# Head decays from running sums in a two-layer trunk kernel: what is computed where, and in which order

## The chip, the cores and the metric

The kernel runs on one core of one Trainium2 chip. The metric is device time in microseconds (us) of one execution, as the median of several runs. The core has five engines that run side by side and meet only at semaphores: TensorE (PE, matmuls; its weight load is shown apart as PEld), VectorE (DVE), ScalarE (ACT), GpSimd (POOL) and SyncE (SP, which here only issues DMAs). TensorE writes its products to PSUM, eight banks of 128 partitions x 512 float32.

## The reference, cut to what matters

Input x is 256 tokens x 2048 channels, and there are two layers (DEPTH = 2). Each layer is

```
h = rmsnorm(x, norm_w)
proj = h @ w_in                      # u, s5_gate, z, xbc, dt, q, k, v, att_gate, merge logits
y_s5  = s5_mixer(u, ...) * silu(s5_gate)
y_ssd = ssd_mixer(z, xbc, dt, ...)
y_att = window_attention(q, k, v, att_gate, ...)
x = x + (sum_b sigmoid(g_b) * (y_b @ w_branch_b)) @ w_out
```

and the part that the change touches most is the decay between two tokens of one head in the ssd mixer (16 heads):

```
dt = softplus(dt_raw + dt_bias)
a = dt * -exp(a_log)                             # [head, token], negative
segsum(a)[l, s] = cumsum(a)[l] - cumsum(a)[s]    # for l >= s, else -inf
scores = (C_l . B_s) * exp(segsum(a))
y = scores @ (x * dt) + ... + x * d_skip
```

The S5 mixer is a diagonal complex recurrence. Its eight tiles of 128 channels need a table of sines and cosines each.

## The kernel before, in words

**Weights as a stream.** All large weights come as 148 slabs per layer (128 x 2048 float32, 1 MB) through four buffers `raw`. SyncE loads slab j+4 once TensorE has done slice j (`load`, L374). ScalarE rounds a slab to `w_hi` (`hi`, L685), VectorE forms the rest `w_lo = raw - w_hi` in the memory of `raw` (`lo`, L1002), and TensorE multiplies three times: high x low, low x high, high x high (`prod3`, L1628). ScalarE and VectorE work three slabs ahead (LEAD = 3). A slice of TensorE is one slab: 48 matmuls of 256 columns (`pair`, L1634) or 24 of 512 columns (`block`, L1661).

**Order by hand.** Every engine's program is written out by slices. What is not the stream (called side work below) is put between the slices of each engine by `if n == ...`, and the engines meet at named marks: `W.wait(LV, "in2")` waits for VectorE's mark `in2` of this layer, `W.wait(MP, "ys1", 1)` for TensorE's mark `ys1` of the tile before. Each engine takes its instructions strictly in its own order, so whatever stands behind a waiting instruction waits too.

**First slices (n = 0 to 15 of a layer).** Slices 0 to 3 give B and C, 4 and 5 k, 6 and 7 v (written to the banks `by` and `bs`), 8 to 15 u. The norm of x is not applied to x: it scales the results. So TensorE starts on unscaled x, sums the squares by a matmul with ones after slice 0 (mark `ss`, L1711; GpSimd adds up the squares in `ssum` before, L498), VectorE and ScalarE make 1/sqrt of it (`rstd`, L1060, L699), and VectorE multiplies each slice's bank with it (mark `in<n>`, L1213). The two banks `mm` take turns, so slice n needs `in<n-2>`. VectorE's side work here: `s5_angles` behind slice 0, `rtok` (token norms turned to columns), `s5_gamma` and `s5_powers` behind slice 2, `c_gamma` behind 3 and 4, `conv` behind 4 to 7, `dt_softplus` (L1163) behind 6. TensorE's `lam_T` (behind slice 5) needs `powers` and `rtok`. GpSimd begins the first S5 tile when `c_gamma` is done (`gamma_end`). SyncE issues, behind the load of j = 13, the store of the first half of u, waits for it to land, and then 17 loads for the first S5 tile: one for `bd`, eight `lam`, eight `ut` (`s5_in`, L380). `kv` (L1756), the first S5 product on TensorE, needs them two slices after slice 15.

**Middle slices (16 to 47)** hold z, xs, q and the attention gate, and four S5 tiles.

**Gate slices (48 to 95).** A loop of four rounds, I = 0 to 3, of 12 slices each. A round holds one S5 tile and two mix tiles c = 0 and 1 (six slices each, t = 0 to 5); a mix tile is two ssd heads and two attention heads. The steps of a mix tile that matter here, before the change:
- VectorE: `conv` of xs and its SiLU `xc` (t = 0); `q_v` and `xdt` (t = 1); a `newton` step on the q norm and `qn` (end of t = 1); then `lo`, `q_c` and `st_make(0)` (t = 2), which multiplies decays `ex` with `gm`; `sc`, maxima and `st_make(1)` (t = 3).
- ScalarE: `sum_decays` (L819) writes three 128 x 128 matrices `m1`, masks scaled with a token's decay, for head 0 at t = 0 and for head 1 at t = 2; `head_exp` (L827) takes exp of what TensorE makes of them; `sines` (L767) of the round's S5 tile at s = 0; `inv_sqrt` at t = 1.
- TensorE: `diff(0)` (L1822) behind t = 2 and `diff(1)` behind t = 3: three float32 products of `m1` with a triangle of ones, which sum the decays between tokens; `ssd_y(0)` and the attention scores `a1(0)` behind t = 3; `a2`, `a3` later.
- GpSimd: `parameters(0)`, the S5 tile of the next round (`s5_tile`, with `values(0)` inside), `parameters(1)`, `values(1)` (L614 to L656). They copy the tile's few numbers into `cur`.
- SyncE: in rounds 0 to 2, behind the load of s = 5, the 17 loads of `s5_in` for the next round.

**Last slices (96 to 147)**: S5 gate, GLU, branch projections, output projection. The change leaves them alone.

## Time and profile before

| | us |
|---|---|
| median of 3 runs | 1973.13 |
| range of the runs | 1972.01 to 6226.87 |
| the profiled execution, its own time | 1972.46 |
| its span, first to last instruction | 1970.7 |
| TensorE matmul busy in it | 1914.7 (97%) |
| VectorE busy | 1335.0 (68%) |
| ScalarE busy | 953.2 (48%) |
| GpSimd busy | 519.0 (26%) |
| mean granted TensorE clock | 0.993 of full speed |

The span is the profiled execution; about 1.8 us lie around it. "Busy" of TensorE counts overlapping matmuls, whose durations are longer than the distance from one start to the next, so cost per matmul is read from start times. The largest of the 6226.87 us is one of the three runs, the other two are within 1.2 us of each other.

### The profile page before, as it was taken

What the parts mean: (1) busy time and instruction counts of PE and PEld (TensorE: products, weight loads), DVE (VectorE), ACT (ScalarE), POOL (GpSimd) and SP (SyncE); (2) the same over time, 40 slices, a digit from 0 to 9 for tenths busy, and PEclk for the clock granted to TensorE, in tenths of its full rate; (3) what the DMA queues carried; (4) which work ended last, traced back from release to release, by engine and by line L of the source; (5) the groups of instructions that cost most, each with busy time, mean ns of one, the idle gap of its engine ahead of it and who ended that gap; (6) DMA issues with size and microseconds to landing.
All of it is one profiled execution on the core that took longest, in us unless ns stands there. A gap on an engine that the chain in (4) does not pass through costs nothing.

```text
span 1970.7 us, 38606 instructions
## 1 busy us (share of the span) xinstructions
PE 1914.7 (97%) x13680; PEld 1706.1 (87%) x13680; DVE 1335.0 (68%) x1733; ACT 953.2 (48%) x1164; POOL 519.0 (26%) x578
## 2 busy tenths in 40 slices
PE   5999999999999999999999999999999999999998
PEld 5999999777777799889999999997777778988898
DVE  6957656777776658666578566667776866676656
ACT  5334333666656554333444344455656565543334
POOL 4215444152342000002312353424241410000033
PEclk9999999999999999999999999999999999999999
DMA  6445555545454447666554555555545454566656
GB/s 259 166 161 206 181 184 189 174 161 190 153 172 166 152 168 256 229 233 211 198 176 168 196 184 178 180 198 174 169 159 173 154 173 171 182 260 234 229 192 207
DMA packets 79444, 372.82 MB, mean 189 GB/s; under 512 B 20560, under 2 KB 27216, under 8 KB 40528
## 3 DMA queue, kind: packets, MB, share of 16 engines
q1 hardware_dynamic: 76560, 359.99, 52.5%
q0 software_dynamic: 1088, 6.80, 0.9%
q10 hardware_dynamic: 1696, 4.72, 0.6%
q8 instruction: 60, 0.98, 0.2%
q14 instruction: 40, 0.33, 0.0%
HBM read 351.80 MB, written 21.76 MB: 190 GB/s over the span
## 4 chain that ended last, share of the span: by engine, by line
PE 83%; DVE 7%; issue 4%; DMA 3%; POOL 1%; ACT 1%; SPq 1%; DVEq 0%; POOLq 0%; ACTq 0%
PE mm L1673 13%; PE mm L1675 13%; PE mm L1674 13%; PE mm L1630 12%; PE mm L1632 12%; PE mm L1631 12%; DMA raw<-in_stream 2%; DVE w_lo L1005 2%; PE by L1836 1%; PE b L1827 1%; PE b L1772 1%; PE b L1848 1%; PE b L1847 1%; POOL ssum L498 1%; DVE qh L1009 1%
## 5 line engine op out<-in xcount | busy, mean ns | idle before, releaser
L691 ACT ACTIVATE w_hi<-raw 128x2048 fp32r<-128x2048 f32 x299 | 571.7, 1913 | 695.8 <-DMA raw<-in_stream 686.3
L1005 DVE TENSOR_TENSOR w_lo<-raw,w_hi 128x2048 fp32r<-128x2048 f32 x299 | 695.9, 2328 | 231.2 <-ACT w_hi L691 222.2
L1630 PE MATMUL mm<-h_lo,w_hi 128*128 128x256 f32 x2240 | 645.6, 288 | 29.6 <-DVE w_lo L1005 15.0
L1632 PE MATMUL mm<-h_hi,w_hi 128*128 128x256 f32 x2240 | 638.6, 285 | 0.0
L1631 PE MATMUL mm<-h_hi,w_lo 128*128 128x256 f32 x2240 | 638.6, 285 | 0.0
L1630 PEld LDWEIGHTS mm<-h_lo,w_hi 128*128 128x128 f32 x2240 | 434.7, 194 | 34.6 <-issue 25.3
L1631 PEld LDWEIGHTS mm<-h_hi,w_lo 128*128 128x128 f32 x2240 | 434.8, 194 | 1.4 <-issue 1.0
L1632 PEld LDWEIGHTS mm<-h_hi,w_hi 128*128 128x128 f32 x2240 | 434.5, 194 | 0.0
L1673 PE MATMUL mm<-w_lo,h_hi 128*128 128x512 f32 x768 | 317.8, 414 | 0.0
L1675 PE MATMUL mm<-w_hi,h_lo 128*128 128x512 f32 x768 | 301.3, 392 | 0.0
L1674 PE MATMUL mm<-w_hi,h_hi 128*128 128x512 f32 x768 | 300.0, 391 | 0.0
L1673 PEld LDWEIGHTS mm<-w_lo,h_hi 128*128 128x128 f32 x768 | 144.5, 188 | 38.1 <-issue 9.4
L672 POOL TENSOR_TENSOR ssum<-ssum,proj 128x256 f32<-128x256 f32 x32 | 73.2, 2289 | 384.7 <-ACT proj L974 357.2
L1675 PEld LDWEIGHTS mm<-w_hi,h_lo 128*128 128x128 f32 x768 | 144.3, 188 | 32.2
L1674 PEld LDWEIGHTS mm<-w_hi,h_hi 128*128 128x128 f32 x768 | 144.8, 189 | 27.2
L1673 PE MATMUL mm<-w_lo,ys 128*128 128x512 f32 x384 | 150.3, 391 | 0.5 <-DVE tmp L1560 0.5
L1675 PE MATMUL mm<-w_hi,ys 128*128 128x512 f32 x384 | 149.5, 389 | 0.0
L1674 PE MATMUL mm<-w_hi,ys 128*128 128x512 f32 x384 | 149.5, 389 | 0.0
L1009 DVE TENSOR_TENSOR proj<-mm,rstd 128x256 f32 (+1 forms) x104 | 47.0, 452 | 134.6 <-PE mm L1632 134.0
L1673 PEld LDWEIGHTS mm<-w_lo,ys 128*128 128x128 f32 x384 | 72.1, 188 | 16.3 <-DVE tmp L1560 0.9
L1675 PEld LDWEIGHTS mm<-w_hi,ys 128*128 128x128 f32 x384 | 72.1, 188 | 15.0
L1674 PEld LDWEIGHTS mm<-w_hi,ys 128*128 128x128 f32 x384 | 72.1, 188 | 14.7
(313 smaller groups left out, 2280.1 us busy)
## 6 DMA issues: line engine op xcount, KB each, us to landing
raw<-in_stream SPq DMA_DIRECT2D x300, 1024.0 KB, 4.8
gscr<-gt SPq DMA_DIRECT2D x48, 256.0 KB, 6.0
gin<-gscr SPq DMA_DIRECT2D x24, 512.0 KB, 5.7
bd<-in_bdense SPq DMA_DIRECT2D x16, 384.0 KB, 5.3
lam<-lscr SPq DMA_DIRECT2D x128, 32.0 KB, 2.7
x_old<-out POOLq DMA_DIRECT2D x2, 2048.0 KB, 9.3
out<-proj ACTq DMA_DIRECT2D x8, 512.0 KB, 6.4
proj<-in_x SPq DMA_DIRECT2D x4, 512.0 KB, 8.5
```

The source lines that it names most:

```text
L498: e.tensor_tensor(ssum[:], ssum[:], proj[:, 16 + m, :], ALU.add).then_inc(x_sum, 1)
L672: e.tensor_tensor(ssum[:], ssum[:], proj[:, bass.ds(I * 4 + (16 + j), 1), :].rearrange("p a b -> p (a b)"), ALU.add).then_inc(x_sum, 1)
L691: e.activation(w_hi[:, j % RAW, :], raw[:, j % RAW, :], ACT.Copy).then_inc(hi_done, 1)
L1005: e.tensor_tensor(w_lo[:, j % RAW, :], raw[:, j % RAW, :], w_hi[:, j % RAW, :].bitcast(F32), ALU.subtract).then_inc(lo_done, 1)
L1009: return e.tensor_tensor(out, a, b, op)
L1630: e.matmul(out, whi, xlo, start=start, stop=False)
L1631: e.matmul(out, wlo, xhi, start=False, stop=False)
L1632: return e.matmul(out, whi, xhi, start=False, stop=stop)
L1673: e.matmul(mm[:, tok, :], xhi[:, rows], w_lo[:, j % RAW, w], start=first and k == 0, stop=False)
L1674: e.matmul(mm[:, tok, :], xhi[:, rows], w_hi[:, j % RAW, w], start=False, stop=False)
L1675: ins = e.matmul(mm[:, tok, :], xlo[:, rows], w_hi[:, j % RAW, w], start=False, stop=last and k == QUAD - 1)
L1772: ins = e.matmul(b4[rows, r * 256 + j * CH:r * 256 + j * CH + CH], bw[rows, r, j * 64:j * 64 + 64], ut[rows, j, :], start=True, stop=True)
```

## The change

1. Behind slice 13 TensorE makes running sums of the decays of all 16 heads at once (four small float32 products into bank `b7`, mark `cs`); ScalarE copies them out, once as rows per head (`csr`, stored to DRAM as `cscr`) and once negated as columns per token (`csb`). In the gate slices GpSimd loads a tile's two rows, spread over all 128 partitions (`crow`, 256 KB per tile, after a wait for VectorE's `dd1` of the tile before), and copies its columns into `cur`. VectorE forms the differences at t = 0 with six instructions (`decays`), ScalarE takes one exp over both heads at t = 1. `sum_decays`, `head_exp` and `diff` go, and `m1` with them; `ex` holds both heads.
2. `sines` in the gate slices moves from s = 0 to s = 2.
3. The product `ss` moves behind slice 1, `rtok` behind slice 3 (on VectorE to n = 4), the rstd work to n = 0 behind `lo`/`hi` of that slice. Slices 2 and 3 write to the banks `by` and `bs`; slices 4 and 5 wait for `in0`, `in1`, slice 6 for `in2` and `in3`.
4. VectorE: `c_gamma` moves from n = 3, 4 to n = 8, 9, `dt_softplus` from n = 6 to n = 11.
5. SyncE: the first S5 tile's `bd` and `lam` loads go behind the load of j = 11, its `ut` loads behind that of j = 15.

The diff, cut to its core:

```diff
@@ SyncE
-                    e.dma_start(bd[:], ob).then_inc(s5_w, 16)
+                    if weights:
+                        e.dma_start(bd[:], ob).then_inc(s5_w, 16)
...
                         e.dma_start(uscr[0:4].rearrange("i p t -> p i t"), proj[:, U:U + 4, :]).then_inc(u_out[0], 16)
+                    if j == 11:
                         e.wait_ge(lam_out, n_lam)
-                        W.settle()
+                        s5_in(0, 0, values=False)
+                    if j == 15:
                         e.wait_ge(u_out[0], n_u)
-                        s5_in(0, 0)
+                        s5_in(0, 0, weights=False)
@@ GpSimd, parameters(c)
+                        MG.mark(e.tensor_copy(cc[:, 5:11].rearrange("p (b d) -> p b d", b=3), csb[:, :, bass.ds(i * 2, 2)]), "cur3")
...
                         MG.mark(e.tensor_scalar(cc[:, 27:28], cc[:, 27:28], 0.5, 0.0, ALU.mult, ALU.add), "cur4")
+                        e.wait_ge(cs_out, e.snap((L + 1) * 16))
+                        W.wait(MV, "dd1", 1)
+                        W.settle()
+                        e.dma_start(crow[:], cscr[bass.ds(i * 2, 2), :].unsqueeze(0).broadcast_to([P, 2, TOK])).then_inc(cs_in, 16)
@@ ScalarE
-                inv_sqrt(LA, "rs", rstd[:], sv[:, 1, :], sv[:, 0, :], lambda: W.wait(LV, "rs_v"))
-
                 nb = start(L, 0)
                 for n in range(16):
                     hi(nb, n + LEAD)
                     if n == 0:
+                        inv_sqrt(LA, "rs", rstd[:], sv[:, 1, :], sv[:, 0, :], lambda: W.wait(LV, "rs_v"))
...
+                    if n == 15:
+                        W.wait(LP, "cs")
+                        LA.mark(e.activation(csr[0:16, :], b7[0:16, 0:TOK], ACT.Copy), "cs_row")
+                        LA.mark(e.activation(csb[:, 0:2, :], b7[:, TOK:TOK + 32].rearrange("p (a b) -> p a b", a=2), ACT.Copy, scale=-1.0), "cs_own")
+                        LA.mark(e.activation(csb[:, 2, :], b7[:, TOK + 32:TOK + 48], ACT.Copy), "cs_rest")
+                        W.wait(LA, "cs_row")
+                        e.dma_start(cscr[:], csr[0:16, :]).then_inc(cs_out, 16)
...
+                        def decay_exp():
+                            W.wait(MV, "dd1")
+                            MA.mark(e.activation(ex[:], ex[:], ACT.Exp), "ex")
...
                             if t == 1:
                                 inv_sqrt(MA, "q", qh[:], rq[:], rv[:], lambda: W.wait(MV, "q_v"))
+                                decay_exp()
...
-                                sum_decays(0)
-                            if s == 0:
+                            if s == 2:
                                 sines()
-                            if t == 2:
-                                head_exp(0)
-                                sum_decays(1)
                             if t == 3:
                                 att_exp(0)
-                                head_exp(1)
@@ VectorE
+                    if n == 0:
+                        lo(nb, LEAD)
+                        W.wait(LP, "ss")
+                        LV.mark(e.tensor_scalar(sv[:, 0, :], b4[:, 0:TOK], 1.0 / D_MODEL, EPS, ALU.mult, ALU.add), "rs_v")
+                        newton(LV, "rs", rstd[:], sv[:, 1, :], sv[:, 0, :])
+                    bank = (by, bs)[n - 2][:, 0:TOK] if n in (2, 3) else mm[:, n % 2, 0:256]
...
-                    if n in (3, 4):
-                        c_gamma(n - 3)
+                    if n in (8, 9):
+                        c_gamma(n - 8)
...
-                    if n == 6:
+                    if n == 11:
                         dt_softplus()
...
+                        def decays():
+                            e.wait_ge(cs_in, turn_in + 16 * c)
+                            W.wait(MG, "cur3")
+                            W.wait(MV, "ST1", 1)
+                            for h in range(2):
+                                for q, (at_r, b) in enumerate(((0, 0), (P, 2), (P, 1))):
+                                    ins = e.tensor_scalar(ex[:, h, q * P:q * P + P], crow[:, h, at_r:at_r + P], cc[:, 5 + 2 * b + h:6 + 2 * b + h],
+                                                          0.0, ALU.add, ALU.min)
+                                MV.mark(ins, f"dd{h}")
...
                                 MV.mark(e.scalar_tensor_tensor(xc[:], tt[:], 1.0, xc[:], ALU.add, ALU.mult), "xc")
+                                decays()
@@ TensorE
+                    if n == 13:
+                        W.wait(LV, "dta")
+                        W.wait(LV, "k_v")
+                        for b in range(2):
+                            e.matmul(b7[0:16, b * P:b * P + P], dta[:, 0, b, :], C("tri", P), start=True, stop=True)
+                        e.matmul(b7[:, TOK:TOK + 32], C("tri", P), dta[:, 0].rearrange("p a b -> p (a b)"), start=True, stop=True)
+                        LP.mark(e.matmul(b7[:, TOK + 32:TOK + 48], C("strict"), dta[:, 0, 0, :], start=True, stop=True), "cs")
...
-                        def diff(h):
-                            W.wait(MA, f"m1_{h}2")
-                            W.wait(MA, f"ex{h ^ 1}", 0 if h else 1)
-                            if not h:
-                                W.wait(MV, "xdt")
-                            e.matmul(b6[:, 0:256], m1[:, 0, :], C("tri"), start=True, stop=False)
-                            e.matmul(b6[:, 128:256], m1[:, 1, :], C("tri", P), start=False, stop=True)
-                            MP.mark(e.matmul(b6[:, 256:384], m1[:, 2, :], C("tri", P), start=True, stop=True), f"diff{h}")
```

The scratch `tq` now shares memory with `rq`, and `xdt` with `tt`, with the waits for it.

## Rows read from the trace of the kernel before

**Rows 1.** The page, part 1: busy time, share of the span, instructions.
```profile
PE 1914.7 (97%) x13680; PEld 1706.1 (87%) x13680; DVE 1335.0 (68%) x1733; ACT 953.2 (48%) x1164; POOL 519.0 (26%) x578
```

**Rows 2.** Waits of TensorE: waiter, releaser, us in total, times, longest.
```profile
PE mm L1630 <- DVE proj L1009: 11.0, 4, 3.7
PE by L1836 <- DVE stt L1009: 10.6, 6, 1.8
PE b L1711 <- POOL ssum L498: 4.5, 1, 4.5
...
PE bs L1788 <- DVE state L1009: 1.4, 1, 1.4
```

**Rows 3.** Windows: length, busy (count) PE, PEld, DVE, ACT, POOL; PEclk; DMA.
```profile
32.40:40.20 7.80, 7.80 (x51) 7.71 (x50) 4.74 (x9) 4.57 (x9) 0.20 (x1) 0.73 0.30 102
1066.70:1085.50 18.80, 18.80 (x144) 18.80 (x145) 14.70 (x15) 9.85 (x8) 0.00 (x0) 0.91 0.35 126
1120.90:1145.50 24.60, 24.60 (x193) 24.60 (x194) 19.64 (x20) 10.64 (x9) 14.43 (x15) 0.93 0.57 193
410.40:421.20 10.80, 10.80 (x42) 8.12 (x43) 7.51 (x17) 3.07 (x10) 2.11 (x2) 0.84 0.22 93
```

**Rows 4.** TensorE's timeline, first slices: start, us, what, idle before and its releaser.
```profile
96.74 0.38 PE L1630 MATMUL mm<-h_lo,w_hi 128*128 128x256 f32 x1 [2.61 <-DVE proj L1009]
150.05 0.38 PE L1630 MATMUL mm<-h_lo,w_hi 128*128 128x256 f32 x1 [1.89 <-DVE proj L1009]
1066.66 0.38 PE L1630 MATMUL mm<-h_lo,w_hi 128*128 128x256 f32 x1 [3.68 <-DVE proj L1009]
1120.88 0.38 PE L1630 MATMUL mm<-h_lo,w_hi 128*128 128x256 f32 x1 [2.80 <-DVE proj L1009]
```

**Rows 5.** VectorE's timeline, first slices of layer 0.
```profile
49.76 0.15 DVE L1232 COPY rtok<-b 128x2 f32<-128x2 f32 x1
...
70.12 0.43 DVE L1158 COPY par<-cw 128x512 f32<-128x512 f32 x1
...
85.59 0.66 DVE L1166 TENSOR_SCALAR sd<-sd 128x32 f32<-128x32 f32 x1
...
90.46 0.19 DVE L1177 SCALAR_TENSOR_TENSOR dta<-sd 128x32 f32<-128x32 f32 x1
```

**Rows 6.** SyncE's issues, layer 0: first of the 17, and the next slabs.
```profile
131.23 0.34 SPq L385 DMA_DIRECT2D bd<-in_bdense  x1
...
140.25 0.93 SPq L377 DMA_DIRECT2D raw<-in_stream  x2
```

**Rows 7.** TensorE's timeline, gate slices, tile c = 1 of round 0.
```profile
398.77 0.59 PE L1827 MATMUL b<-cst,m 128*128 128x256 f32 x2
399.20 0.38 PE L1828 MATMUL b<-cst,m 128*128 128x128 f32 x2
399.43 0.39 PE L1829 MATMUL b<-cst,m 128*128 128x128 f32 x2
399.65 1.31 PE L1782 MATMUL bs<-proj,kb 128*128 x8
...
410.39 0.64 PE L1836 MATMUL by<-stt,xdt 128*64 128x256 f32 x2 [1.77 <-DVE stt L1009]
```

**Rows 8.** VectorE's timeline, two tiles of round 0: c = 0, then c = 1.
```profile
357.32 2.28 DVE L1005 TENSOR_TENSOR w_lo<-raw,w_hi 128x2048 fp32r<-128x2048 f32 x1
...
400.63 0.43 DVE L1009 TENSOR_TENSOR rq<-qh 128x256 f32<-128x256 f32 x1 [1.17 <-ACT qh L703]
...
405.03 3.37 DVE L1005 TENSOR_TENSOR w_lo<-raw,w_hi 128x2048 fp32r<-128x2048 f32 x1
...
409.19 1.07 DVE L1009 TENSOR_TENSOR stt<-ex,gm 128x384 f32<-128x384 f32 x1
```

**Rows 9.** GpSimd's timeline, round 0: the next S5 tile, start and end.
```profile
387.80 0.19 POOL L505 COPY cur<-s5p 128x12 f32 x1 [0.18 <-POOL cur L631]
...
409.80 0.72 POOL L573 COPY dec<-cur 128x252 f32<-128x252 f32 x1
```

**Rows 10.** The view of DMA issues: KB each, median us from issue to landing.
```profile
kcur<-kscr POOLq DMA_DIRECT2D x16, 64.0 KB, 5.5
```

**Rows 11.** VectorE's timeline: an instruction with one input in SBUF.
```profile
336.15 0.28 DVE L1340 TENSOR_SCALAR t<-t 128x256 f32<-128x256 f32 x1
```

More of the change, by code:

```diff
@@ L191, in program @@
         xc = sb("xc", [P, TOK])
+        o_tt = top[0]
         tt = sb("tt", [P, TOK])
-        xdt = sb("xdt", [P, 2, 2, 64])
-        m1 = sb("m1", [P, 3, P])
-        ex = sb("ex", [P, 384])
+        xdt = at("xdt", [P, 2, 2, 64], F32, o_tt)
+        ex = sb("ex", [P, 2, 384])
+        crow = sb("crow", [P, 2, TOK])
+        csb = sb("csb", [P, 3, 16])
         stt_ = sb("stt", [P, 384])
@@ L379, in _, with s5_in @@
             with e.Fori(0, DEPTH) as L:
-                def s5_in(I, more):
+                def s5_in(I, more, weights=True, values=True):
                     W.settle()
@@ L608, in _ @@
                 W.wait(LV, "prep_end")
-                W.wait(LA, "prep_end")
+                W.wait(LA, "cs_rest")
                 W.wait(LP, "k_rot")
@@ L817, in _ @@
                         cc = cur[:, c, :]
-                        def sum_decays(h):
-                            W.wait(MG, "cur1")
-                            W.wait(MP, "diff0" if h else "diff1", 0 if h else 1)
-                            for q, (nm, b) in enumerate((("strict", 0), ("ones", 1), ("strict", 1))):
-                                MA.mark(e.activation(m1[:, q, :], C(nm), ACT.Copy, scale=cc[:, 16 + 2 * b + h:17 + 2 * b + h]),
-                                        f"m1_{h}{q}")
-                        def head_exp(h):
-                            W.wait(MP, f"diff{h}")
-                            W.wait(MV, "ST1" if h == 0 else "ST0", 1 if h == 0 else 0)
-                            MA.mark(e.activation(ex[:], b6[:, 0:384], ACT.Exp), f"ex{h}")
+                        def decay_exp():
+                            W.wait(MV, "dd1")
+                            MA.mark(e.activation(ex[:], ex[:], ACT.Exp), "ex")
                         def att_exp(h):
@@ L862, in _ @@
                             if t == 0:
-                                W.wait(MP, "q_ss", 1)
+                                W.wait(MV, "qh", 1)
                                 MA.mark(e.activation(tq[:], proj[:, bass.ds(i + Q, 1), :], ACT.Square), "q_sq")
@@ L1058, in _ @@
                 W.layer(L)
-                W.wait(LP, "ss")
-                LV.mark(e.tensor_scalar(sv[:, 0, :], b4[:, 0:TOK], 1.0 / D_MODEL, EPS, ALU.mult, ALU.add), "rs_v")
-                newton(LV, "rs", rstd[:], sv[:, 1, :], sv[:, 0, :])
                 count = [0]
@@ L1425, in _ @@
                                 W.wait(MP, "xT")
-                                W.wait(MP, "ys1", 1)
+                                W.wait(MV, "xc")
                                 W.wait(MG, "cur1")
@@ L1632, in prod3, with pair @@
                 return e.matmul(out, whi, xhi, start=False, stop=stop)
-            def pair(nb, j, before=None, after=None):
+            def pair(nb, j, before=None, after=None, out=None):
                 e.wait_ge(lo_done, nb + (j + 1 + RAW))
@@ L1641, in pair @@
                     w = slice(k * P, k * P + P)
-                    ins = prod3(mm[:, j % 2, 0:256], w_hi[:, j % RAW, w], w_lo[:, j % RAW, w], h_hi[:, k, :], h_lo[:, k, :],
+                    ins = prod3(mm[:, j % 2, 0:256] if out is None else out, w_hi[:, j % RAW, w], w_lo[:, j % RAW, w], h_hi[:, k, :], h_lo[:, k, :],
                                 k == 0, k == KT - 1)
@@ L1692, in _ @@
                 for n in range(16):
-                    if n in (2, 3, 4, 5):
-                        W.wait(LV, f"in{n - 2}")
+                    if n in (4, 5):
+                        W.wait(LV, f"in{n - 4}")
+                    if n == 6:
+                        W.wait(LV, "in2")
+                        W.wait(LV, "in3")
                     if n >= 8:
@@ L1705, in _ @@
                     else:
-                        pair(nb, n, first if n == 0 else None)
-                    if n == 0:
+                        pair(nb, n, first if n == 0 else None, out=(by, bs)[n - 2][:, 0:TOK] if n in (2, 3) else None)
+                    if n == 1:
                         e.wait_ge(const_in, 16)
@@ L1893, in _ @@
                                 W.wait(MV, "xc")
-                                W.wait(MA, "ex1", 1)
+                                W.wait(MV, "xdt", 1)
                                 for a in range(2):
@@ L1897, in _ @@
                                 MP.mark(ins, "xT")
-                            if t == 2:
-                                diff(0)
                             if t == 3:
@@ L1902, in _ @@
                                 a1(0)
-                                diff(1)
                             if t == 4:
```

33 lines of the change are left out of this document (20 added, 13 removed).

## The prediction

> **What bounds the kernel.** I read the page's busy times first. TensorE's matmuls are busy 1914.7 of 1970.7 us [rows 1], and VectorE, the next, 68%. So nearly every us of TensorE work that goes is a us of the kernel, as long as the others keep up. Then the waits of TensorE [rows 2]: besides the start of the kernel and the last layer's edge there are only four kinds. 4.5 us wait for `ssum` (once), 11.0 us for VectorE's reading of a bank (four times), 10.6 us for `stt` in the gate slices (six times, at most 1.8 each), and 1.4 us for `state`. The timeline places the four waits of the second kind [rows 4]: at slice 10 (2.61 and 3.68 us in layers 0 and 1) and at the first slice behind `kv` (1.89 and 2.80 us). Last, the granted clock in windows behind these waits [rows 3]: it is 0.73 of full speed for 7.80 us behind the `ssum` wait, 0.91 for 18.80 us behind slice 10 in layer 1, 0.93 for 24.60 us behind `kv` in layer 1, and 0.84 for 10.80 us behind the `stt` wait of layer 0, round 0. 1.0 is 2.4 GHz, and slow matmuls there run at 1.2 GHz. Length times (1 - clock) is the cost of a dip: 2.1, 1.7, 1.7 and 1.7 us. I take 1.7 for layer 0's slice 10 too. The other five `stt` waits and layer 0's `kv` I count without one.
>
> **The gate slices: what goes from TensorE.** `diff` is three float32 products. From the start of the first to the start of what follows are 398.77 to 399.65 = 0.88 us [rows 7]. 2 layers x 8 tiles x 2 heads = 32 of them: 28.2 us, all on the engine that bounds.
>
> **The six waits for stt.** They stand in tile c = 1 of rounds 0 to 2. `stt` for head 0 comes at 409.19 + 1.07, and TensorE goes on at 410.39 [rows 7, 8]. One might think that `stt` waits for `diff` and its exp. It does not there: it stands behind a `lo` that began at 405.03 [rows 8], and behind the q norm before it. That chain starts with a slab whose load SyncE issues only behind the 17 loads of `s5_in` (rounds 0 to 2 have them, round 3 does not and has no wait). The change leaves these loads where they are. TensorE arrives 0.88 us sooner (no `diff(0)`), so with an unchanged VectorE the wait is 1.77 + 0.88 = 2.65 us, and `diff(0)` brings nothing in these six tiles.
>
> VectorE's chain is stretched while GpSimd works: `lo` takes 3.37 us at 405.03 against 2.28 us at 357.32, when GpSimd has nothing [rows 8]. GpSimd's S5 tile runs from 387.80 to 410.52 [rows 9]. The change holds it back: `parameters(0)` now waits for `dd1` of the running tile. `xc` is done at about 392, six subtractions follow, so the S5 tile starts some 8 us later, at about 396, and ends at about 418. It still covers 400 to 410, but with its short steps rather than the 128x512 ones. The unknown is how far this stretches VectorE. From below: all stretch gone, which is 1.1 us on `lo` and about 3 us on the seven instructions around it, and no wait. From above: as in the trace, 2.65 us, and up to 1.0 us more for the softmax chain of head 0, which falls under GpSimd's later end. I take a wait of 1.4 us, nearer to the trace since GpSimd is busy there all the same. Six tiles: 10.6 + 1.7 (the dip) = 12.3 us before, 8.4 after, 3.9 gained.
>
> A rule stands beside this. The Trainium skill ("SBUF — State Buffer", Who interferes with whom) says that a VectorE instruction with two SBUF inputs and a GpSimd instruction that reads SBUF hold one port pair in turn, whole instruction by whole instruction, and that who issues first decides. The `lo` of 3.37 us agrees. By that rule alone the later S5 tile would block VectorE as before, which is the first rival below.
>
> **What the gate slices get.** VectorE's six subtractions read 128 columns each; the nearest row is 0.28 us for 256 columns [rows 11], so 6 x 0.28 = 1.7 us at most and some 1 us likely, per tile, at t = 0 behind `xc`. They stand ahead of `q_v` and `xdt`. In c = 1 the next `lo` moves from 397.2 to about 398 at worst, and the `newton` behind it waits for ScalarE's `inv_sqrt` until 400.63 anyway [rows 8]: nothing on the path. If that cover goes, 16 x 1 us = 16 us. ScalarE loses six scaled copies and two exps and gets one exp over 768 columns; `sines` at s = 2 brings another table change ahead of `gate`, which at s = 3 waits for TensorE and has four slices for it. Nothing waits. The `crow` load is on GpSimd's queue, behind `dd1` of the tile before; a load like it lands in 5.5 us [rows 10], and it has some 44 us until the next tile's t = 0. It costs GpSimd one issue. GpSimd's own next due time (`kv` at s = 3 of the next round) is some 38 us after its new end. Nothing on the path.
>
> **The first slices.** What goes: the `ssum` wait (4.5) with its dip (2.1), since TensorE now does slice 1 in between (it ends at 33.0, the squares are in at 31.7) and slices 2 and 3 have their own banks; the waits at slice 10 (2.6 + 3.7) with dips (1.7 + 1.7); the waits behind `kv` (1.9 + 2.8) with layer 1's dip (1.7); the wait for `state` (1.4). Sum 24.1 us. Slice 10's waits go because VectorE reads `in8` late, behind `dt_softplus`, which runs from 85.59 to 90.65, 5.1 us, and `c_gamma`, which ends at 70.12 + 0.43 [rows 5]. Both are moved behind the narrow place: 9.4 us of VectorE work, while TensorE comes some 6 us sooner. At n = 11 `dt_softplus` ends near 110 to 114, `cs` asks for `dta` near 114. `kv`'s waits go because SyncE was busy with 17 loads from 131.23 and issued the next two slabs at 140.25 [rows 6]; split, 9 loads (4.5 us) go behind j = 11, where each slab still has two slices of slack, and 8 (3.8 us) behind j = 15, landing some 4 us before `kv`. GpSimd's first S5 tile starts at `gamma_end`, 24 us later, and is done some 20 us before `kv`.
>
> What comes: the `cs` products, four, of which the two long ones cost 0.23 us each like the second product of `diff` [rows 7], together about 0.9 us, twice 1.8. And new waits: VectorE serves `rtok` at n = 4, behind `s5_powers`, `lo` 6 and `lo` 7. Followed in layer 0, VectorE gets there at 64.1 and TensorE asks for it (`lam_T`) at 63.2. Before, it was ready at 49.76 [rows 5]. I take 1.0 us per layer, between 0 and 2.5 (VectorE as late as in the trace). In layer 1 the product with `wdt_lo` waits about 1.1 us as rstd comes 6 us later. 3.1 us together. First slices: 24.1 - 1.8 - 3.1 = 19.2 us.
>
> **Sum.** 28.2 + 3.9 + 19.2 = 51.3 us. The profiled execution took 1972.46 us (its span 1970.7 and 1.8 around it), which stands 0.7 us under the median of 1973.13. So 1972.46 - 51.3 = 1921 us.
>
> **Rivals.**
> *The wait for stt grows.* For: the chain that ends in it is not in the diff, and TensorE comes sooner. Against: GpSimd's heavy steps move out of it. Wait and softmax 3.65 us in six tiles is 21.9 us, and dips behind half of them 5.1: 27.0 instead of 12.3, so the gate slices give 13.5 and the time is 1940. Chance 0.20.
> *The first slices only move their waits.* VectorE has the same work there, and in layer 0 it is busy nearly without a gap from 37 to 102 us; if rstd's chain and `rtok` hold TensorE 4 us per layer and the clock dips, 4 us are left of 19: 1936. For: `rtok` and `wdt_lo` come within 1 us of TensorE. Against: 9.4 us moved away ahead of slice 10. Chance 0.12.
> *All waits go.* 28.2 + 12.3 + 24.1 - 1.8 = 62.8: 1910. It needs GpSimd's shift to free VectorE. Chance 0.12.
> *Slower: VectorE waits for crow at t = 0.* `decays` stands ahead of `lo`, so a late `crow` stops the stream in each of 16 tiles. To pass 2% slower (2012) TensorE must stand 5.7 us per tile, beyond the some 10 us that the slabs are ahead: `crow` would have to land near 60 us after its issue, against 5.5 for `kcur` [rows 10]. With 6.5 us per tile: 1921 + 104 = 2025. Chance 0.05. The Trainium skill ("SBUF — State Buffer", SBUF: two separate sides) names a mechanism for such lateness: a DMA issued by GpSimd is starved of descriptors while VectorE runs in a two-port mode, 3100 instead of 620 ns. No row here shows it, and 2.5 us would still be covered.
>
> **Chances and range.** The forecast, 0.51, with its own range 1908 to 1934 (`stt` waits between 0 and 2.7 us, `lam_T` 0 to 2.5, dips 0 to 3 more). The range for 8 in 10 takes in most of the first two rivals and of the third: 1905 to 1945. 2% of 1973.13 is 39.5 us, about what a measurement of this kernel can tell from no change; the border is 1933.7. Below it lie the forecast's case but its edge, and the third rival and a small part of the first two: 0.72. Within 2%: 0.23. Slower: 0.05.
>
> **What would show it.** Right: no `m` products on TensorE, its busy time about 28 us less; no `ssum` wait; slice 10 and the slice behind `kv` start without waiting; `lam_T` waits about 1 us; `stt` waits in six tiles of 1 to 2 us; no wait of VectorE for `crow`. Wrong: `stt` waits above 2.5 us or in other tiles; a new wait of TensorE for `w_lo` or `qn` at t = 1 or 2, from the subtractions; `a2` waiting for ScalarE; `cs` waiting for `dta`; dips of the clock behind them.

## The result, and the profile after

| | us, median (lowest to highest) |
|---|---|
| before | 1972.57 (1971.90 to 6226.87) |
| after | 1937.12 (1934.26 to 1939.86) |
| after / before | 0.9824 [0.9809, 0.9839] |
| forecast | 1921, range 1905 to 1945 |

One run of the kernel before, at 6226.87 us, stands far off the others and is not in the ratio. The time is in the range, 16 us above the forecast. Of the 51.3 us forecast the change gave 35.5. It stayed within 2% of the kernel before, where I had put 0.23 of the chance; I had put 0.72 on more than that. The profiled execution took 1937.21 us (span 1935.3).

The page, part 1, after:

```profile
PE 1885.4 (97%) x13504; PEld 1676.6 (87%) x13504; DVE 1340.1 (69%) x1829; ACT 935.6 (48%) x1066; POOL 530.4 (27%) x610
```

TensorE is busy 29.3 us less than in [rows 1]; the 32 `diff` were costed at 28.2. The two figures are not quite of one kind: the busy time after holds the eight `cs` products of the two layers, and both hold slow matmuls. Its waits after (waiter, releaser, us in total, times, longest):

```profile
PE mm L1654 <- DVE w_lo L1014: 14.9, 1, 14.9
PE b L1772 <- DVE dta L1182: 9.2, 2, 4.9
PE by L1861 <- DVE stt L1018: 6.6, 6, 1.1
PE b L1879 <- ACT pt L862: 1.9, 6, 0.3
...
PE b L1784 <- DVE kk L1278: 1.4, 2, 1.0
PE b L1654 <- DVE wdt_lo L1018: 1.1, 1, 1.1
...
PE bs L1822 <- DVE state L1018: 1.0, 1, 1.0
```

Against [rows 2]: the waits for `proj` (11.0) and `ssum` (4.5) are gone and those for `stt` are down from 10.6 to 6.6. A wait that was not there before stands in second place: the first product of `cs` waits for `dta`, 9.2 us in two layers.

**The gate slices.** TensorE's timeline at the first `kv` product of a round: of two successive rounds of layer 0, first before, then after.

```profile
456.49 1.15 PE L1772 MATMUL b<-ut,bw 64*64 64x64 f32 x32
...
545.64 1.15 PE L1772 MATMUL b<-ut,bw 64*64 64x64 f32 x32
```

```profile
448.89 1.15 PE L1806 MATMUL b<-ut,bw 64*64 64x64 f32 x32
...
533.99 1.15 PE L1806 MATMUL b<-ut,bw 64*64 64x64 f32 x32
```

A round takes 85.10 instead of 89.15 us. The six rounds that can be read off so are shorter by 3.9 to 4.4 us, 4.06 in the mean. Of that 3.52 are the four `diff` (4 x 0.88), 0.66 the shorter wait for `stt` and 0.25 that for `qn`, less 0.3 for `pt`. Eight rounds at that rate are 32.5 us, and the forecast had 28.2 + 3.9 = 32.1. 32.5 is a little high, as the last round of each layer has no such waits.

**The first slices.** That leaves some 3 us for them, where the forecast had 19.2. TensorE in layer 0 after, behind slice 13:

```profile
121.10 1.03 PE L1772 MATMUL b<-cst,dta 128*16 128x128 f32 x4 [4.91 <-DVE dta L1182]
122.06 0.64 PE L1773 MATMUL b<-dta,cst 128*128 128x32 f32 x2
122.51 0.59 PE L1774 MATMUL b<-dta,cst 128*128 128x16 f32 x2
122.93 0.56 PE L1654 MATMUL mm<-h_lo,w_hi 128*128 128x256 f32 x1
```

What it waits for is the last step of `dt_softplus`. VectorE in that stretch:

```profile
109.75 2.26 DVE L1014 TENSOR_TENSOR w_lo<-raw,w_hi 128x2048 fp32r<-128x2048 f32 x1
111.94 0.61 DVE L1171 TENSOR_SCALAR sd<-sd 128x32 f32<-128x32 f32 x1
...
114.30 4.76 DVE L1177 SCALAR_TENSOR_TENSOR sd<-sd 128x32 f32<-128x32 f32 x7
...
119.44 0.52 DVE L1179 TENSOR_SCALAR sd<-sd 128x32 f32<-128x32 f32 x1
...
120.78 0.19 DVE L1182 SCALAR_TENSOR_TENSOR dta<-sd 128x32 f32<-128x32 f32 x1
```

From 111.94 to 120.97 are 9.0 us, where [rows 5] have 5.1. Seven of the steps stand in one row, 4.76 us. The same seven before the change (VectorE's timeline of the kernel before):

```profile
87.99 1.55 DVE L1172 SCALAR_TENSOR_TENSOR sd<-sd 128x32 f32<-128x32 f32 x7
```

In the mean a step of 0.22 us has become one of 0.68. GpSimd in the stretch after, its first S5 tile:

```profile
96.58 0.94 POOL L610 MEMSET cz<- 128x1024 f32 x1 [62.18 <-DVE par L1163]
...
110.02 2.49 POOL L564 TENSOR_TENSOR cl<-par,pw 128x256 f32 x1 [0.18 <-POOL cl L569]
112.69 0.65 POOL L567 TENSOR_TENSOR tA<-par,pw 128x256 f32 x1 [0.18 <-POOL cl L564]
113.42 0.81 POOL L569 TENSOR_TENSOR cl<-cl,tA 128x256 f32<-128x256 f32 x1
114.50 1.30 POOL L575 TENSOR_TENSOR bw<-bd,lam 128x512 f32<-128x512 f32 x1 [0.27 <-POOL cl L569]
115.88 1.32 POOL L577 TENSOR_TENSOR bd<-bd,lam 128x512 f32<-128x512 f32 x1
117.27 0.72 POOL L579 TENSOR_TENSOR bw<-bw,bd 128x256 f32<-128x256 f32 x1
117.95 0.72 POOL L580 TENSOR_TENSOR bw<-bw,bd 128x256 f32<-128x256 f32 x1
118.62 0.39 POOL L584 COPY dec<-cur 128x252 f32<-128x252 f32 x1
118.95 0.19 POOL L587 COPY cur<-par 128x1 f32 x1
```

Read the two together. While VectorE does its seven steps, from 114.30 to 119.06, GpSimd begins six instructions, so VectorE gets about one short step done per instruction of GpSimd. The price goes both ways: the `cl` product at 110.02 takes 2.49 us under the `w_lo` of 109.75, and another of the same form takes 0.65.

How the tile came to lie there is seen in the kernel before. GpSimd's timeline, the last step of its tables and what comes next:

```profile
87.12 0.80 POOL L558 TENSOR_TENSOR cl<-cl,tA 128x256 f32<-128x256 f32 x1
141.23 1.29 POOL L564 TENSOR_TENSOR bw<-bd,lam 128x512 f32<-128x512 f32 x1 [53.32 <-DMA lam<-lscr]
```

The tile began at 70.71 and `dt_softplus` at 85.59, 14.9 us later; after the change it is 96.58 and 111.94, 15.4 us. So the moves of `c_gamma` and of `dt_softplus` left the two almost as they stood to each other. Before, the tile lay over the first steps of the chain too (the first took 0.66 us, and 0.16 in e3_pool_late below), but at 87.92 GpSimd stopped to wait for the `lam` loads, and the seven steps began at 87.99 with nothing beside them. After, these loads are issued from 102.12 on, GpSimd goes on without a stop at 114.50, and its instructions lie over the seven steps of 114.30. By these rows it is the move of SyncE's loads that let them. This is read from the traces of both layers (GpSimd's wait for `lam` is 54.22 us in layer 1) and not shown by a run: none has the loads alone in their old place.

The granted clock falls during the wait. Windows after (length, busy of PE, PEld, DVE, ACT, POOL, then the granted clock), layer 0 from slice 13 to `kv`, then slices 11 to 13 of layer 1 with `cs`:

```profile
106.86:147.81 40.95, 35.06 (x260) 33.42 (x258) 30.57 (x42) 12.58 (x14) 16.12 (x20) 0.92 0.52 170
```

```profile
1060.00:1078.70 18.70, 14.07 (x92) 12.55 (x91) 17.95 (x28) 5.75 (x3) 16.41 (x19) 0.83 0.56 181
```

Length times (1 - clock): 3.3 and 3.2 us. A part of it falls into the waits for `dta` themselves, where a slow clock costs nothing:

```profile
116.19:121.10 4.91, 0.00 (x1) 0.01 (x1) 4.49 (x10) 0.00 (x0) 4.28 (x8) 0.88 0.77 200
1070.31:1074.55 4.24, 0.00 (x1) 0.01 (x1) 3.93 (x10) 0.00 (x0) 3.82 (x7) 0.73 0.65 184
```

That is 0.6 and 1.1 us, so some 5 us are left for the slow `cs` products and the matmuls behind them. With the 9.2 us for `dta` and 1.4 for `kk`, which stands under the same tile, that is 15 us.

### The profile page after: what moved, and what is told of

It reads as the page before. It is cut to its first block, busy times and chain, and to the rows that moved or that the text cites. A ratio compares the mean times of both kernels' runs of the same rounds, so it can differ in the third digit from the quotient of the medians.

```text
span 1935.3 us, 38244 instructions
## 1 busy us (share of the span) xinstructions
PE 1885.4 (97%) x13504; PEld 1676.6 (87%) x13504; DVE 1340.1 (69%) x1829; ACT 935.6 (48%) x1066; POOL 530.4 (27%) x610
## 4 chain that ended last, share of the span: by engine, by line
PE 74%; DVE 8%; POOL 5%; issue 5%; DMA 3%; ACT 3%; POOLq 0%; DVEq 0%; ACTq 0%; SPq 0%
PE mm L1654 12%; PE mm L1655 12%; PE mm L1656 12%; PE mm L1697 10%; PE mm L1699 9%; PE mm L1698 9%; DMA raw<-in_stream 2%; DVE w_lo L1014 2%; ACT w_hi L706 1%; POOL cl L564 1%; PE b L1806 1%; POOL tB L540 1%; POOL ssum L509 1%; POOL cl L569 1%; PE bs L1816 1%
## 5 line engine op out<-in xcount | busy, mean ns | idle before, releaser
L1654 PE MATMUL mm<-h_lo,w_hi 128*128 128x256 f32 x2176 | 625.1, 287 | 18.3 <-DVE w_lo L1014 14.9
L1655 PE MATMUL mm<-h_hi,w_lo 128*128 128x256 f32 x2176 | 619.2, 285 | 0.0
L1656 PE MATMUL mm<-h_hi,w_hi 128*128 128x256 f32 x2176 | 619.0, 284 | 0.0
L1654 PEld LDWEIGHTS mm<-h_lo,w_hi 128*128 128x128 f32 x2176 | 421.0, 193 | 22.7 <-issue 18.4
L1655 PEld LDWEIGHTS mm<-h_hi,w_lo 128*128 128x128 f32 x2176 | 421.0, 193 | 0.9 <-issue 0.5
L1656 PEld LDWEIGHTS mm<-h_hi,w_hi 128*128 128x128 f32 x2176 | 420.9, 193 | 0.0
L1697 PEld LDWEIGHTS mm<-w_lo,h_hi 128*128 128x128 f32 x768 | 144.1, 188 | 41.7 <-issue 12.1
L1699 PEld LDWEIGHTS mm<-w_hi,h_lo 128*128 128x128 f32 x768 | 144.1, 188 | 32.1
```

What stands on the lines that cost most here:

```text
L1654: e.matmul(out, whi, xlo, start=start, stop=False)
L1655: e.matmul(out, wlo, xhi, start=False, stop=False)
L1656: return e.matmul(out, whi, xhi, start=False, stop=stop)
L1697: e.matmul(mm[:, tok, :], xhi[:, rows], w_lo[:, j % RAW, w], start=first and k == 0, stop=False)
L1699: ins = e.matmul(mm[:, tok, :], xlo[:, rows], w_hi[:, j % RAW, w], start=False, stop=last and k == QUAD - 1)
```

## The experiments

All ratios are to the kernel before, run on the same chip.

| kernel | us | ratio |
|---|---|---|
| e1_softplus6 | 1924.89 | 0.9745 [0.9728, 0.9761] |
| e2_cs15 | 1936.74 | 0.9809 [0.9792, 0.9825] |
| e3_pool_late | 1921.93 | 0.9738 [0.9722, 0.9754] |
| e4_first_only | 1967.94 | 0.9958 [0.9944, 0.9972] |
| e5_first_held | 1955.80 | 0.9908 [0.9885, 0.9931] |
| e9_decays_only | 1940.56 | 0.9841 [0.9825, 0.9858] |
| e6_split_s5_loads | 1924.91 | 0.9754 [0.9737, 0.9772] |
| e7_crow_in_tile | 1935.75 | 0.9813 [0.9796, 0.9830] |
| e8_tile_behind_stt | 1926.22 | 0.9773 [0.9755, 0.9791] |
| e10_behind_stt_split | 1924.02 | 0.9759 [0.9743, 0.9775] |
| e11_before_behind_stt | 1965.24 | 0.9954 [0.9934, 0.9974] |
| e12_tile_between | 1926.62 | 0.9767 [0.9746, 0.9789] |

### What cost the first slices their gain

**e1_softplus6**, the changed kernel with `dt_softplus` back in its old place:

```diff
-                    if n == 11:
+                    if n == 6:
                         dt_softplus()
```

> The changed kernel, with dt_softplus back behind n = 6 (c_gamma stays at 8 and 9). In the changed kernel TensorE waits 4.9 and 4.2 us at the cs products for dta, the products take 1.8 instead of 0.9 us, and some 1.9 and 1.4 us go by slow matmuls behind them. Theory A (dta comes late because its chain runs at n = 11 under GpSimd's first S5 tile, 9.0 us against 5.1 before the change): no wait at cs, time 1937 - 13 = 1924. The read of slice 8's bank, which is 5.4 us ahead of TensorE now, takes up the 5 us. Theory B (VectorE simply has too much work in the first 16 slices, wherever it stands): the waits at slice 10 come back, 2 to 4 us per layer with their dips, and the time is 1931 to 1935.

1924.89 us, 12 us under the changed kernel, as theory A had it. The wait for `dta` is gone and VectorE's seven steps, at 78.37, take 1.55 us. TensorE now waits 3.4 us in all for `kk`, whose chain still lies under the tile: its last step takes 1.01 us, and 0.75 in e3_pool_late.

**e2_cs15**, the `cs` products two slices later:

```diff
-                    if n == 13:
+                    if n == 15:
                         W.wait(LV, "dta")
```

> The changed kernel, with the cs products behind slice 15 instead of 13. Both theories: dta is ready 11 us before it is asked for, no wait, products at full clock, time about 1924. If instead the products' place is not what costs (the wait only moves, to a later slab or to ScalarE's copies behind slice 15), the time stays at 1934 to 1937.

A miss for both theories; what came true is the third outcome written down, the wait that only moves: 1936.74 us, the time of the changed kernel. TensorE does not wait for `dta` any more. It waits as long for VectorE's reading of slice 12's bank, which stands behind `dt_softplus` on VectorE:

```profile
121.48 0.57 PE L1654 MATMUL mm<-h_lo,w_hi 128*128 128x256 f32 x1 [4.89 <-DVE proj L1018]
```

So the place of `cs` is not the cause. The late chain is, whoever asks for its end.

**e3_pool_late**, GpSimd's first S5 tile held until `dt_softplus` is through:

```diff
-                W.wait(LV, "gamma_end")
+                W.wait(LV, "dta")
                 W.settle()
                 LG.mark(e.memset(cz[:], 0.0), "cz0")
```

> The changed kernel, with GpSimd's first S5 tile held until dta is made (it waited for c_gamma). Nothing of TensorE or VectorE is moved. Theory A (contention between VectorE and GpSimd stretches the chain): the seven steps of the chain take 1.6 us again instead of 4.8, kn comes 1 us sooner, cs waits less than 1 us, time about 1924 to 1926; kv is not late, since GpSimd has 20 us to spare. Theory B (the place at n = 11 is too late by itself): cs still waits 3 us or more per layer, time 1934 or more.

1921.93 us, under theory A's 1924 to 1926. By the ratios (0.9738 against 0.9824) it is 17 us under the changed kernel, by the medians 15. No instruction of VectorE was moved, and its seven steps are back at the old length:

```profile
108.68 0.16 DVE L1171 TENSOR_SCALAR sd<-sd 128x32 f32<-128x32 f32 x1
...
109.93 1.55 DVE L1177 SCALAR_TENSOR_TENSOR sd<-sd 128x32 f32<-128x32 f32 x7
...
112.62 0.19 DVE L1182 SCALAR_TENSOR_TENSOR dta<-sd 128x32 f32<-128x32 f32 x1
```

The chain takes 4.1 us, 4.9 less than in the changed kernel, and it starts at 108.68 instead of 111.94, since the steps ahead of it (`w_lo` at 102.02 and `kk`) are no longer stretched either. `cs` starts at 114.61 with no wait and takes 1.0 us instead of 1.8, and the window from 102.5 to 142.0 has a clock of 1.00. The S5 tile, now from 113, is in time for TensorE with nothing to spare: `dec` is made at 138.85, and TensorE begins its first product with the tile at 138.84. Expected were 20 us of slack. This run shows contention as the cause, and the forecast was that of a kernel without it.

**e4_first_only** is the kernel before with the first-slice part alone: the product `ss` behind slice 1, own banks for slices 2 and 3, `c_gamma` at n = 8 and 9, `dt_softplus` at n = 11, the split loads. `diff` stays and there is no `cs`. **e5_first_held** is the same with GpSimd held as in e3_pool_late.

> The kernel before with the first-slice parts alone: ss behind slice 1, own banks for slices 2 and 3, c_gamma at 8 and 9, dt_softplus at 11, the loads of the first S5 tile split. No cs products, diff stays. Theory A: the first slices are worth what was forecast for them, less the terms for cs: 24.1 - 3.1 = 21 us, time about 1952. Theory B: they give only the 3 us that they gave in the changed kernel, time about 1969.

> The kernel before with the first-slice part of the change alone (norm behind slice 2 with banks of its own, c_gamma at n = 8 and 9, dt_softplus at n = 11, S5 loads split), the decays left as they were, and GpSimd held until the last step of dt_softplus before its first S5 tile. Theory A (the only thing that ate the forecast gain of the first slices is GpSimd's moved tile lying over VectorE's short steps): the two 4.9 us waits for slice 12's bank go, the seven-step chain is back at 1.5 to 1.6 us, and the time is 1951 to 1957, 19 us under the kernel before, which was the forecast's term. Rival B (the moved work costs its gain in other ways too): the waits go elsewhere and the time stays over 1962.

```diff
-                    if n in (3, 4):
-                        c_gamma(n - 3)
+                    if n in (8, 9):
+                        c_gamma(n - 8)
...
-                    if n == 6:
+                    if n == 11:
                         dt_softplus()
```

e4_first_only gains 0.4%, 1967.94 us where theory B had 1969: slice 14 waits 4.87 us behind `dt_softplus` although no `cs` is there to ask for `dta`, and the seven steps take 4.48 us. Held, it is 1955.80 us, 17.8 under the kernel before. Its interval, 13.6 to 22.7 us, holds the forecast's term, which is 21.0 without the `cs` products. Holding GpSimd has a price: TensorE waits 2.4 us in all for `dec` of the late tile, at the first S5 products of the two layers.

**e9_decays_only** is the other part alone: running sums, subtractions, one exponential a tile, `cs` at n = 13, the sines two slices on; the first slices are those of before.

> The kernel before with the decay part of the change alone (cs products at n = 13, running sums, subtractions on VectorE, one exponential a tile, no diff products; the S5 sines two slices on), the first slices left as they were. Theory A (the gate slices give 32 us by themselves, and the products of cs cost 1 to 2 us a layer and wait for nothing, since dta is ready by n = 6): 1941 to 1946, with no wait for dta. Rival B (the two parts give the same time twice, and the decays alone show the gain of the whole change and no less): 1936 to 1939. Rival C (the products lengthen the clock dip of slices 10 to 13 in each layer): over 1948.

```diff
+                            def decays():
+                                e.wait_ge(cs_in, turn_in + 16 * c)
+                                W.wait(MG, "cur3")
...
-                            W.wait(MA, f"ex{h}")
+                            W.wait(MA, "ex")
...
-                            if t == 2:
-                                diff(0)
```

1940.56 us, 33.0 under the kernel before, just below theory A's band, with no wait for `dta`. 33.0 + 17.8 = 50.8 us, e3_pool_late gains 52.6, and the forecast's sum was 51.3: the two parts add up, as long as GpSimd is out of the way.

### What the place of GpSimd's tile is worth in the gate slices

TensorE still waits 6 x 1.1 us for `stt`. These kernels build on e3_pool_late, but for e11_before_behind_stt.

**e6_split_s5_loads**, SyncE's 17 small loads in two lots:

```diff
-                        if s == 5 and more:
+                        if s == 4 and more:
                             W.wait(SP, "KV")
-                            s5_in(I, 5)
+                            s5_in(I, 5, values=False)
+                        if s == 5 and more:
+                            s5_in(I, 5, weights=False)
```

> The changed kernel with GpSimd held until dta, and SyncE's 17 small loads for the next S5 tile in the gate slices split: the 9 of the weights behind the load of slice 4, the 8 of u behind that of slice 5. Theory A (TensorE's six waits for stt, 1.1 us each, start with the load of slice 6, which is issued some 3 us late behind the 17 loads, and end as a late w_hi, w_lo and stt): the six waits fall under 0.3 us each and the time is 1914 to 1917. Rival B (the late load is hidden, and stt is late because it stands behind w_lo on VectorE in any case): the waits stay and the time is 1920 to 1924. Rival C (the nine loads make another slab late): a new wait for w_lo or h_lo appears and the time is 1922 or over.

The `stt` waits go, so the late slab did start that chain. Nothing is won: 1924.91 us, in the range of rival C, though by other waits than it named. The waits come back one step on, behind the softmax:

```profile
PE b L1881 <- ACT pr L859: 6.2, 6, 1.0
PE b L1881 <- ACT pt L864: 3.9, 6, 0.7
PE mm L1699 <- DVE tmp L1586: 3.2, 2, 1.7
```

**e7_crow_in_tile**, the load of `crow` moved from ahead of the S5 tile into `values`, so that the tile no longer stands behind VectorE's subtractions:

```diff
                     def parameters(c):
...
-                        e.wait_ge(cs_out, e.snap((L + 1) * 16))
-                        W.wait(MV, "dd1", 1)
-                        W.settle()
-                        e.dma_start(crow[:], cscr[bass.ds(i * 2, 2), :].unsqueeze(0).broadcast_to([P, 2, TOK])).then_inc(cs_in, 16)
                     def values(c):
...
+                        i = I * 2 + c
+                        e.wait_ge(cs_out, e.snap((L + 1) * 16))
+                        W.wait(MV, "dd1", 1)
+                        W.settle()
+                        e.dma_start(crow[:], cscr[bass.ds(i * 2, 2), :].unsqueeze(0).broadcast_to([P, 2, TOK])).then_inc(cs_in, 16)
```

> The changed kernel with GpSimd held until dta, and its load of crow moved from ahead of each S5 tile of the gate slices to the middle of it, so that the tile no longer waits until VectorE has read crow. GpSimd's tile then starts 5 to 6 us sooner against TensorE. Theory A (the place of GpSimd's tile against VectorE's w_lo sets how long the six stt waits are, as the forecast's step had it): they come back to between 1.8 and 2.6 us each and the time is 1926 to 1931. Rival B (the place of GpSimd's tile is worth nothing there): they stay at 1.0 to 1.2 us and the time is 1920 to 1924.

1935.75 us, 14 us more than e3_pool_late, worse even than theory A, which had the `stt` waits right (1.8 us each) and none for `qn`. Waits of TensorE:

```profile
PE by L1862 <- DVE stt L1019: 10.6, 6, 1.8
PE b L1902 <- DVE qn L1507: 8.7, 6, 1.5
```

VectorE's chain in round 0, first of this kernel, then of e3_pool_late:

```profile
392.50 1.29 DVE L1507 SCALAR_TENSOR_TENSOR qn<-proj,par,qh 128x256 f32<-128x256 f32 x1 [0.25 <-DVE qh L1019]
393.72 3.37 DVE L1015 TENSOR_TENSOR w_lo<-raw,w_hi 128x2048 fp32r<-128x2048 f32 x1
...
397.88 1.07 DVE L1019 TENSOR_TENSOR stt<-ex,gm 128x384 f32<-128x384 f32 x1
```

```profile
390.82 0.54 DVE L1506 SCALAR_TENSOR_TENSOR qn<-proj,par,qh 128x256 f32<-128x256 f32 x1 [0.25 <-DVE qh L1018]
391.28 2.81 DVE L1014 TENSOR_TENSOR w_lo<-raw,w_hi 128x2048 fp32r<-128x2048 f32 x1
...
394.81 1.02 DVE L1018 TENSOR_TENSOR stt<-ex,gm 128x384 f32<-128x384 f32 x1
```

What lies over `qn` and the start of `w_lo` decides. Here it is GpSimd's two longest instructions, as in the kernel before; 3.37 and 1.07 are the numbers of [rows 8]:

```profile
392.25 1.26 POOL L575 TENSOR_TENSOR bw<-bd,lam 128x512 f32<-128x512 f32 x1 [0.28 <-POOL cl L569]
393.59 1.34 POOL L577 TENSOR_TENSOR bd<-bd,lam 128x512 f32<-128x512 f32 x1
```

`w_lo` starts at 393.72 and stands until the second of them ends at 394.93; the 2.16 us that are left are about its own length, 2.28. In e3_pool_late the tile starts 13.4 us ahead of `stt` instead of 21.5, and these two come at 396.70 and 398.05, behind `stt`. The six rounds of this kernel that can be read off are 14.8 us longer in all than those of e3_pool_late, so the whole loss lies there. The wait of GpSimd for `dd1`, a side effect of the `crow` load, is thus worth 14 us of the change's 32 in these slices.

**e8_tile_behind_stt**, the tile held until VectorE has made the second `stt`; **e11_before_behind_stt**, the same line in the kernel before; **e10_behind_stt_split**, with the split loads of e6_split_s5_loads as well; **e12_tile_between**, held until the first `stt` only (`"ST0"`):

```diff
                     W.wait(MG, "cur4")
+                    W.wait(MV, "ST1", 1)
                     s5_tile(L, I, 4, lambda: values(0))
```

> The changed kernel with GpSimd held until dta in the first slices, and in the gate slices held until VectorE has made the tile's second stt (at 403.7 in the run without this) before it starts the next S5 tile (now at 381). Theory A (what is left of the six waits for stt, 1.1 us, and of those for pt, 0.3 us, is GpSimd's S5 tile over VectorE's chain from q's norm over w_lo to stt; behind that chain it meets nothing on which TensorE waits): both waits go and the time is 1912 to 1916. Rival B (the tile then lies over the next slices' w_lo and convolution, and TensorE waits there): new waits of 1 us or more, six times, and the time is 1920 to 1926. Rival C (w_lo stands ahead of stt on VectorE, whatever GpSimd does): the stt waits stay and the time is 1920 to 1923.

> As the kernel with GpSimd's gate tile behind the second stt, with SyncE's 17 small loads split over slices 4 and 5 as well. Without GpSimd's later tile the split kept TensorE off stt but put 1.0 us waits for ACT's pr and 0.7 us for pt in their place (1924.9). Theory A (those came from the softmax chain on VectorE under GpSimd's tile too): they go and the time is 1910 to 1914. Rival B (the nine loads of the weights delay the slab of slice 5 and so ACT's order): the waits for pr and pt stay near 6 and 4 us in all and the time is 1920 to 1926.

> The kernel before, with one wait added: in the gate slices GpSimd starts an S5 tile only when VectorE has made the second stt of the tile before. It tells how much of the gate slices' gain is the place of GpSimd's tile alone. Theory A (the six stt waits of 1.77 us and the qn waits of 0.25 us are GpSimd's tile over VectorE's chain, which the change shifted by 6 us as a side effect of the crow load): both go, 12 us, and the time is 1959 to 1964. Rival B (they are due to the order on VectorE): the time is 1970 to 1975.

> As the kernel with GpSimd's gate tile held until the second stt, but held until the first stt only (made at 394.5 there), so that its 23 us lie from 395 to 418, between the two places that cost before: VectorE's chain from q's norm to the first stt (ended 395) and its convolution (from 417). Theory A (what the tile costs is set by which of VectorE's chains it lies over, and TensorE waits for nothing of what VectorE makes in between): neither waits for stt nor for xc, at most 0.5 us each, and the time is 1913 to 1918. Rival B (the softmax of the second head lies in between and TensorE waits for it instead): waits for pr, pt or the second stt of about 1 us six times and the time is 1920 to 1925. Rival C (each tile's 23 us slow VectorE by the same amount wherever they lie): 1922 to 1926.

In e8_tile_behind_stt `w_lo` is back at 2.29 us and `stt` at 0.55, and TensorE waits for neither `stt` nor `pt`. Rival B came true: the tile lies over the convolution of the next tile, six times 1.9 us. The wait, and VectorE's three steps of that convolution in this kernel, then in e3_pool_late:

```profile
PE b L1922 <- DVE xc L1472: 11.3, 6, 1.9
```

```profile
419.40 3.21 DVE L1191 SCALAR_TENSOR_TENSOR xc<-proj,cur,xc 128x255 f32<-128x255 f32 x3
```

```profile
418.48 1.90 DVE L1190 SCALAR_TENSOR_TENSOR xc<-proj,cur,xc 128x255 f32<-128x255 f32 x3
```

e10_behind_stt_split shows the same 11.2 us for `xc` and no wait for `pr` or `pt`; its time misses theory A for the reason that e8's does. e11_before_behind_stt gains 7 us where 12 were expected: 12.1 us of waits for `stt` and `qn` go, 8.5 us for `xc` come. What gives the other 4 us was not traced. In e12_tile_between the tile lies between the two chains. Four rounds of six are the shortest of all (84.2 us against 85.1), but two take 86.5. TensorE waits for `pt` six times (3.9 us in all), twice 1.5 us for `stt` and twice 0.5 us for `xc`. So theory A missed, and rival B came true in part. Apart from that, the held first tile is late for `bs` in the first slices (`dec`, 2.6 us). The time, 1926.62, is no better than the others', and its interval overlaps with e3_pool_late's. Why it stands 5 us above e3_pool_late, though TensorE's waits in the two profiles add up to about the same, is open.

No place that I tried beats e3_pool_late, which is 0.9738 [0.9722, 0.9754] of the kernel before and some 0.9% under the changed kernel. It has the lowest time of all runs, but the intervals of e1, e6, e10 and e12 overlap with its own.

## Why the prediction was right, and where it was wrong

The measured 1937 us lies in the range and 16 us above the sum. Nearly all of this distance comes from one term. That the time is still in the range is owed to rivals of another mechanism, which had pushed the upper bound to 1945: the second had the first slices lose their gain too, and gave 1936, but by rstd's chain and `rtok` holding TensorE 4 us per layer. `rtok` held it 0.3 us, once. So the agreement with that number is luck.

**The `diff` products, 28.2 us: right.** A round is 4.06 us shorter, of which four `diff` at 0.88 make 3.52, and the rest is what the waits give.

**The `stt` waits, 12.3 to 8.4 us: right in size, 1.1 us each for a forecast of 1.4,** and right in mechanism: the wait for `dd1` shifts GpSimd's tile by the 8 us forecast (its start is 21.4 us ahead of `stt` in [rows 8, 9] and 392.44 to 405.56 = 13.1 after), and what lies over the chain are the tile's short instructions. e7_crow_in_tile is the first rival's world, the chain covered as before: 3.2 us a tile, where I had bounded it by 2.65 and 1.0 for the softmax. The sum shows only the 3.9 us that the shift gains. What it avoids is larger: e7_crow_in_tile without it is 14 us slower, and the first rival had priced that at 19 (1940 against 1921). The change does not aim at this shift, but the prediction foresaw it.

**What the gate slices get: right.** Six subtractions take 1.26 us (forecast 1 to 1.7) and nobody waits for them; `crow` lands in 5.4 us in the median and TensorE never stands for it. New are six waits of 0.3 us for ScalarE's `pt`.

**The first slices, what goes: right.** No wait for `ssum`, at slice 10 or behind `kv`. TensorE waits 1.1 us for `wdt_lo` as forecast, but in layer 0 and not in layer 1; for `rtok` 0.3 us in layer 0 and nothing in layer 1, instead of 1.0 in each. A wait for `state` of 1.0 us stays where none was forecast.

**The first slices, what comes: wrong, by 16 us.** The step that failed is the pair of sentences "At n = 11 `dt_softplus` ends near 110 to 114, `cs` asks for `dta` near 114" and "GpSimd's first S5 tile starts at `gamma_end`, 24 us later, and is done some 20 us before `kv`". The first carried the 5.1 us of [rows 5] to the new place, where the chain takes 9.0 and ends at 121. Without GpSimd beside it (e3_pool_late) it takes 4.1 and ends at 112.8, within the forecast's 110 to 114. The second counted GpSimd's moved work against GpSimd's own due time alone. And the move of SyncE's loads was weighed for the slabs and for `kv` only. In the trace of before GpSimd stood from 87.92 to 141.23 for `lam`, and that is why the chain's seven steps were short there; with the loads behind j = 11 it does not stand. The other half of the evidence was in my hands: [rows 8] show a `w_lo` of 3.37 us under the same tile, and I used it for `stt` only. "`cs` waiting for `dta`" stood in the list of what would show the forecast wrong, with no price. Its price was 9.2 us, and some 6 more for `kk`, the slow `cs` and the dips behind it: 15 us. e3_pool_late gives back 15 by the medians, 17 by the ratios.

The rule of the Trainium skill ("SBUF — State Buffer", Who interferes with whom) was weighed against `w_lo` alone. It holds in the first slices too: steps with two inputs in SBUF take 0.68 instead of 0.22 us when GpSimd reads SBUF beside them. That the engine that comes second stands until the other's instruction is through agrees with the two `w_lo`: the one of 109.75 began first and kept its 2.26 us, and the one of e7_crow_in_tile came second and took 3.37. Read as a rule about any VectorE work under GpSimd, it would have added one instruction of GpSimd, 0.7 to 1.3 us, to each of the seven short steps, an estimate of 5 us or more; 3.2 were measured (4.76 against 1.55).

## What to carry to other kernels

When VectorE or GpSimd work is moved, lay the two engines' timelines over each other at the new place before taking a duration from the old one: a chain of short dependent VectorE steps cost about one GpSimd instruction per step here, three times its own length. Look also at what GpSimd was waiting for at the old place. A load that comes earlier takes away a pause under which other work was fast. A wait added on GpSimd's queue is a change of schedule for VectorE, for good or ill (14 us here), so try the tile's start as a knob by itself. When moving the consumer of a late value changes nothing, look for what else is queued behind the value on its engine.

## What the runs showed of the hardware

- Seven dependent 128x32 steps on VectorE: 1.55 us in every kernel in which no instruction of GpSimd's S5 tile lies beside them, 4.76 and 4.48 us under it (layers 0 and 1). A step with one input there (L1179) takes 0.52 us in layer 0, and 0.18 without the tile, so it is not only steps with two inputs that are slowed.
- GpSimd's 128x256 product takes 0.65 us, and 2.49 with a `w_lo` of 2.26 us beside it, which itself is then not slowed. In e7_crow_in_tile it is VectorE's `w_lo` that is slowed, 3.37 for 2.28 us: an instruction of GpSimd was already under way when it began.
- The four `cs` products take 1.8 us behind a wait of 4.9 us, at a granted clock of 0.50, and 1.0 us without a wait, at 1.00.
